# Output projection by column halves, routing tile by tile, and the slot table between the first expert's gate and up

## The reference, cut to what matters

```python
x = x + mixer(rmsnorm(x, norm_mix_w[layer]), ...)        # ends with: return mixed @ w_out
x = x + hierarchical_moe(rmsnorm(x, norm_ffn_w[layer]), ...)

g_logits = hf @ w_router_group + b_router_group          # 4 groups: argmax and softmax weight
e_logits = hf @ w_router_expert + b_router_expert        # 32 experts: 8 in the chosen group
top_v, top_i = lax.top_k(e_in_group, 2)                  # two experts for each token
weights = g_w * jax.nn.softmax(top_v)
a = jax.nn.silu(xblk @ w_expert_gate[e]) * (xblk @ w_expert_up[e])   # width 512
y = a @ w_expert_down[e]                                 # scattered back, times its weight
```

## Time and profile before

| what | us |
|---|---|
| median of three runs | 1530.46 (1529.99 to 1534.29) |
| the profiled execution | 1531.19 |
| its span, first to last instruction | 1529.2 |
| PE busy | 1479.4 (97%) |
| VectorE, ScalarE, GpSimd busy | 824.6, 346.5, 259.4 |
| mean granted TensorE clock | 0.995 |

### The profile page before, as it was taken

One profiled execution on the slowest core, in us unless ns is written; L12 is line 12 of the kernel. 1 busy time (PEld: TensorE's weight loads), 2 busy tenths in 40 slices (PEclk: granted clock), 3 DMA queues, 4 the chain that ended last, 5 costly groups with the idle time before them and its releaser, 6 DMA issues.

```text
span 1529.2 us, 23483 instructions
## 1 busy us (share of the span) xinstructions
PE 1479.4 (97%) x9358; PEld 929.7 (61%) x9358; DVE 824.6 (54%) x1530; ACT 346.5 (23%) x684; POOL 259.4 (17%) x153
## 2 busy tenths in 40 slices
PE   8999999999999999999999999998999999999996
PEld 6877767665555555544488777685655555554453
DVE  2267773555555555454534687635555555555456
ACT  6335563100000000000163354711000000000002
POOL 3343322010000000000133422401000000000001
PEclk9999999999999999999999999999999999999998
DMA  6442144799999999999833321449999999999995
GB/s 206 101 101 69 42 165 179 288 413 422 425 422 424 421 424 421 424 423 422 338 112 94 83 70 28 166 192 392 418 425 420 426 420 423 422 424 421 424 424 223
DMA packets 105773, 464.04 MB, mean 303 GB/s; under 512 B 16616, under 2 KB 59880, under 8 KB 72640
## 3 DMA queue, kind: packets, MB, share of 16 engines
q1 hardware_dynamic: 98208, 449.13, 73.4%
q0 software_dynamic: 6112, 12.32, 2.1%
q10 hardware_dynamic: 1344, 1.05, 0.2%
HBM read 464.32 MB, written 6.29 MB: 308 GB/s over the span
## 4 chain that ended last, share of the span: by engine, by line
PE 79%; DMA 17%; DVE 3%; issue 1%; DVEq 0%; ACTq 0%
PE bank L1755 23%; DMA area<-in_w_expert_up_dram 16%; PE bank L1771 11%; PE bank L1731 7%; PE bank L1578 5%; PE bank L1583 5%; PE bank L1582 5%; PE bank L1648 2%; PE bank L1650 2%; PE bank L1506 2%; PE bank L1649 2%; PE bank L1507 2%; PE bank L1508 2%; PE bank L1598 2%; PE bank L1620 1%; DVE area L1382 1%
## 5 line engine op out<-in xcount | busy, mean ns | idle before, releaser
L1755 PE MATMUL bank<-area 128*64 128x256 f32 x4096 | 461.7, 382 | 17.0 <-DMA area<-in_w_expert_up_dram 15.6
L1755 PEld LDWEIGHTS bank<-area 128*64 128x64 f32 x4096 | 288.5, 137 | 184.6 <-issue 25.8
L1128 DVE TENSOR_TENSOR xres<-xres,bank 128x512 f32<-128x512 f32 x512 | 316.4, 679 | 5.2 <-PE bank L1731 5.2
L1771 PE MATMUL bank<-area 128*64 128x512 f32 x1024 | 233.8, 598 | 6.3 <-DVE area L1382 1.5
L737 POOL DMA_INDIRECT area<-rows,gath x62 | 70.0, 1129 | 739.1 <-PE bank L1723 699.5
L1360 DVE TENSOR_TENSOR area<-area,bank 128x256 f32<-128x256 f32 x64 | 27.0, 421 | 292.9 <-PE bank L1755 292.9
L712 POOL TENSOR_TENSOR w_lo<-area,w_hi 128x1024 fp32r<-128x1024 f32 x55 | 135.1, 2458 | 274.4 <-ACT w_hi L809 274.4
L975 ACT ACTIVATE y_hi<-bank,slot_w 128x512 fp32r<-128x512 f32 x64 | 44.1, 689 | 579.7 <-PE bank L1771 579.7
L1771 PEld LDWEIGHTS bank<-area 128*64 128x64 f32 x1024 | 67.8, 136 | 131.1 <-issue 109.6
L1578 PE MATMUL bank<-h_hi,w_hi 128*128 128x512 f32 x336 | 135.0, 402 | 0.0
L1583 PE MATMUL bank<-h_hi,w_lo 128*128 128x512 f32 x320 | 124.9, 390 | 0.0
(11 more groups left out here) (194 smaller groups left out, 1680.2 us busy)
## 6 DMA issues: line engine op xcount, KB each, us to landing
area<-in_w_expert_up_dram SPq DMA_DIRECT2D x64, 2048.0 KB, 27.4
area<-in_w_expert_gate_dram SPq DMA_DIRECT2D x64, 2048.0 KB, 25.9
area<-in_w_expert_down_dram SPq DMA_DIRECT2D x64, 2048.0 KB, 26.7
area<-in_w_in_dram SPq DMA_DIRECT2D x58, 512.0 KB, 3.9
area<-in_w_out_dram SPq DMA_DIRECT2D x4, 2048.0 KB, 11.2
rows<-area POOLq DMA_DIRECT2D x8, 512.0 KB, 6.7
area<-in_decay_dram SPq DMA_DIRECT2D x2, 1024.0 KB, 6.3
out_dram<-area SPq DMA_DIRECT2D x4, 512.0 KB, 2.9
```

The costliest lines, as they stand in the source:

```text
L1128: tt(xs, xs, bank[4 + i][:, :], ALU.add).then_inc(s_sa[i], 1)
L1755: last = mm(bank[i][SLOTS * half:SLOTS * (half + 1), 0:256], xT[:, c % 4, c // 4, :], w[:, i, c, 256 * half:256 * (half + 1)], start=(c == ...
L1771: last = mm(bank[into][SLOTS * half:SLOTS * (half + 1), :], hx[:, c % 2, c // 2, :], w[:, c, 512 * half:512 * (half + 1)], start=(c == 0), ...
```

## The change

The projection runs by column halves: half 0 of all four tiles, then half 1 of each. Half 0's transposes and logits stand in between; ScalarE copies half 0's transposes and VectorE half 1's. ScalarE sums the squares of each half by itself and scales the rows of all four tiles. When a tile has its logits, `choose` picks its experts by 14 chained VectorE steps on that tile alone; its ranks and its part of the first expert's rows are made on PE as it comes (`rank`, `xb` with a tile number), a tile or two behind. What remains after the last half are steps of tiles 2 and 3, four fillers instead of five and a half, and the count. The slot table follows expert 0's gate. `route`, which prepares it, follows the taking of expert 0's input on VectorE. Buffers move in the area, two of the gather buffers now lie on `xn2` of tile 0, and GpSimd clears them after `xb`. SyncE's part is not changed.

```diff
@@ areas
-XN0 = (PT0, PT0 + D, PB0, PB0 + D)
...
+XN0 = (XG0, OH0, YH0, YH0 + D)
@@ steps
-    out += [("begin", 0, 1), ("mh", 7), ("ml", 7), ("begin", 1, 0), ("begin", 1, 1)]
-
-    out += [("wo", 0, 0), ("wo", 0, 1), ("wo", 1, 0), ("wo", 1, 1)]
-    between = [[("fT", 0, 0)], [("fT", 0, 1)], [("lg", 0, 0)],
-               [("lg", 0, 1)], [("fT", 1, 0)], [("fT", 1, 1)],
-               [("lg", 1, 0)], [("fT", 2, 0), ("lg", 1, 1)], [("fT", 2, 1)],
-               [("lg", 2, 0), ("fT", 3, 0)], [("lg", 2, 1)], [("lg", 3, 0)]]
+    out += [("begin", 1, 0), ("mh", 7), ("ml", 7), ("begin", 2, 0), ("begin", 3, 0)]
+
+    out += [("wo", 0, 0), ("wo", 1, 0), ("fT", 0, 0), ("wo", 2, 0), ("fT", 1, 0), ("lg", 0, 0)]
+    out += [("wo", 3, 0), ("fT", 2, 0), ("lg", 1, 0)]
+    between = [[("fT", 3, 0), ("lg", 2, 0)], [("lg", 3, 0)], []]
+    for t in range(1, NT):
+        between += [[("fT", t - 1, 1)],
+                    [("rank", t - 2), ("lg", t - 1, 1)] if t > 1 else [("lg", t - 1, 1)],
+                    [("xb", t - 2)] if t > 1 else []]
     for n, small in enumerate(between):
-        out += [("wp", 2 + n // 6, n // 3 % 2, n % 3), *small]
+        out += [("wp", n // 3, 1, n % 3), *small]
         if n % 3 == 2:
-            out += [("wo", 2 + n // 6, n // 3 % 2)]
-    out += [("fT", 3, 1), ("lg", 3, 1), ("rank",), ("xb",), ("table",), ("wtab",)]
+            out += [("wo", n // 3, 1)]
+    out += [("rank", 2), ("fT", 3, 1), ("xb", 2), ("lg", 3, 1), ("rank", 3), ("xb", 3), ("count",)]
+    out += [("table",), ("wtab",)]
@@ banks
-            s, b = s[:2], 2 + s[1] % 2
+            s, b = s[:2], (2, 3, 6, 7)[s[1]]
...
-        elif kind == "begin" and s[1]:
-            b = 2 + s[2]
+        elif kind in ("begin", "wp", "wo"):
+            b = s[1] % 2 if s[2] else s[1]
@@ GpSimd
-                nc.gpsimd.memset(at(XG0 + 512, 2 * 512), 0.0).then_inc(s_xgz, 1)
+                pool.wait_ge(s_rows[0], 16 * (layer + 1))
+                is_full(pool, ("xb",), layer)
+                nc.gpsimd.memset(at(XG0, 2 * 512), 0.0).then_inc(s_xgz, 1)
@@ ScalarE
+                    elif kind == "wo" and s[2] == 0:
+                        t = s[1]
+                        is_taken(act, s, layer)
+                        link(nc.scalar.activation(xn2[t][:, 0:512], xres[:, t, 0:512], ACT.Square,
+                                                  accum_out=stat[:, 4 + t:5 + t]))
...
+                    elif kind == "fT" and s[2] == 0:
+                        b, n = result(s, layer)
+                        is_full(act, s, layer)
+                        nc.scalar.activation(hT2[s[1] % 2], bank[b][:, :].rearrange("p (c t) -> p c t", c=4), ACT.Copy
+                                             ).then_inc(freed[b], 2)
@@ VectorE
+            def choose(layer, t):
+
+                g_log, e_log = lgt[:, t, 0:NG], lgt[:, t, NG:].rearrange("p (g e) -> p g e", g=NG)
...
+                link(red(gm, g_log, AX.X, ALU.max))
+                link(stt(out=gfi, in0=g_log, scalar=gm, in1=k("g"), op0=ALU.is_equal, op1=ALU.mult))
+                link(red(own_group, gfi, AX.X, ALU.min))
+                link(ts(pen, k("g"), own_group, NEG, ALU.not_equal, ALU.mult))
+
+                link(tt(near.rearrange("p (g e) -> p g e", g=NG), e_log, each(pen, EPG), ALU.add))
+                link(red(top, near, AX.X, ALU.max))
...
+            def first_rows(layer):
+
+                for kth, found in enumerate((in1, in2)):
+                    link(tt(a12f[:, kth, :, :], over(k("x"), NT), each(found, NE), ALU.is_equal))
+                tt(ed, m2, m1, ALU.subtract).then_inc(s_rin, 1)
+                tt(gs, lgt[:, :, 0:NG], each(gmax, NG), ALU.subtract).then_inc(s_rin, 1)
...
@@ VectorE, the steps
-                        if t and half:
-                            ffn_rows(layer, t - 1)
...
-                        if t == NT - 1:
-                            is_taken(dve, s[:2], layer)
-
-                route(layer)
+                        is_taken(dve, s[:2], layer)
+                        choose(layer, t)
+                    elif kind == "rank":
...
+                        link(nc.vector.tensor_copy(rank[:, t, :], bank[b][:, 0:NE]))
+                        dve.sem_inc(freed[b], 2)
+                        ts(hot_first[t], k("slot")[:, 0:SLOTS], rank[:, t, 0:1], chosen[:, t, 0:1].bitcast(F32),
+                           ALU.is_equal, ALU.mult).then_inc(s_first_hot, 1)
+
+                first_rows(layer)
...
                 take_input(0)
-                for t in range(NT):
-                    dve.wait_ge(s_rows[t], 16 * (layer + 1))
-                b, n = result(("table",), layer)
-                rows_of(layer, ("table",), 0, NE).then_inc(freed[b], 1)
-                weigh(layer)
+                route(layer)
@@ PE
+                        for u in range(t):
+                            mm(o[:, 0:NE], sums[:, 1, :], chosen[:, u, :], start=(u == 0), stop=False)
+                        last = mm(o[:, 0:NE], sums[:, 0, :], chosen[:, t, :], start=(t == 0), stop=True)
+                    elif kind == "count":
+                        for t in range(NT):
+                            last = mm(o[:, 0:NE], sums[:, 1, :], chosen[:, t, :], start=(t == 0), stop=(t == NT - 1))
...
                     if s == ("lg", NT - 1, 1):
-                        is_taken(pe, ("lg", NT - 2), layer)
-                        unread(2, 512, 512, 512, 512, 512, 256)
+                        is_taken(pe, ("wo", NT - 2, 1), layer)
+                        unread(0, 512, 512, 512, 512)
...
                     def ahead(part):
+                        if part and e == 0:
+                            slots_by_expert()
                         if part and e == NE - 1:
                             spread_block(e - 1, (0, 1))
...
-                slots_by_expert(range(0, 3))
                 first_transpose()
-                slots_by_expert(range(3, TOPK * NT))
```

More of the change, by code:

```diff
@@ new lines, in first_rows @@
+            def first_rows(layer):
[3 more added lines that the diff above has]
+                tt(gs, lgt[:, :, 0:NG], each(gmax, NG), ALU.subtract).then_inc(s_rin, 1)
+                b, n = result(("xb",), layer)
+                is_full(dve, ("xb",), layer)
+                for half in range(2):
+                    own = slice(256 * half, 256 * (half + 1))
+                    nc.vector.tensor_copy(xg[0][:, own], bank[b][:, own]).then_inc(freed[b], 1)
@@ L1110, in route @@
                        ).then_inc(s_hots, 1)
-                link(nc.vector.tensor_copy(wbig, each(nfe[:, layer, :].rearrange("p (h j) -> p j h", h=2), SLOTS)))
-                dve.wait_ge(s_rows[1], 16 * (layer + 1))
-                b, n = result(("xb",), layer)
-                is_full(dve, ("xb",), layer)
-                for half in range(2):
-                    own = slice(256 * half, 256 * (half + 1))
-                    nc.vector.tensor_copy(xg[0][:, own], bank[b][:, own]).then_inc(freed[b], 1)
+                tt(hot_exp[:, :, :], a12f.rearrange("p k t e -> p (k t) e"), each(k("row"), NE), ALU.mult
+                   ).then_inc(s_tabin, 1)
+                b, n = result(("count",), layer)
+                is_full(dve, ("count",), layer)
+                nc.vector.tensor_copy(cnt, bank[b][:, 0:NE]).then_inc(freed[b], 2)
+                weigh(layer)
+                for t in range(NT):
+                    dve.wait_ge(s_rows[t], 16 * (layer + 1))
+                b, n = result(("table",), layer)
+                rows_of(layer, ("table",), 0, NE).then_inc(freed[b], 1)
             def add_spread(layer, e, t):
@@ L1462, in _, with table @@
             ident = k("ident")
-            def table(o, hot_col, n, ready=None, part=range(TOPK * NT)):
-                for i in part:
+            def table(o, hot_col, n, ready=None):
+                for i in range(TOPK * NT):
                     if ready is not None and i % NT == 0:
```

182 lines of the change are left out of this document (81 added, 101 removed).

## The result

| | before | after |
|---|---|---|
| median, us | 1531.48 (1529.99 to 1534.29, 6 runs) | 1541.56 (1540.14 to 1544.61, 6 runs) |
| profiled execution / its span | 1531.19 / 1529.2 | 1543.27 / 1541.2 |
| mean granted clock | 0.995 | 0.991 |

The ratio is 1.0066, with a 95% interval of 1.0052 to 1.0081. Forecast was 1528.9, within 1524.5 to 1535.0: wrong in sign, and outside the range. In this part T is read at the issue of the load that waits for it.

A forecast was written before the change was run, and what follows sets the result against it. The experts were taken as bound by the weight stream, which would end 0.8 us earlier in each layer, 1.6 in all: 1531.19 - 1.6 = 1529.6, against the median 1528.9. The range was 1524.5 to 1535.0.

The forecast's parts named there:

- T: The moment the last half is projected, in the first layer: 287.58 us before, forecast at 290.9.
- What bounds the kernel: Experts: bound by the weight stream, 14.8 us per expert against about 13.9 for PE; the stream never pauses.
- The head start: Start of the weight stream: two gate loads leave 20 us earlier; the last load lands 4.1 us earlier, if T stays.
- T does not stay: Projection: rows, ranks, shape changes and bank waits ahead of T move it by 3.3 us, between 2.2 and 4.8.
- the two bank waits: Projection: logits of tiles 0 and 1 wait for banks, about 0.4 us twice, 0.8 in all.
- the 0.4 of the ranks: Projection: ranks newly ahead of T, three matmuls of 0.14 us, cost 0.4 us.
- Tail from T to g: Routing tail behind the projection: 11.5 us instead of 16.2, with 14 choosing steps in 3.0 us.
- g: The first gate matmul, in the first layer: 303.74 us before, forecast at 302.4, 1.3 earlier.
- Table between gate and up: Expert 0: table's 1.2 us on PE free; gather starts at g + 6.0, takes 5.0 us, PE waits 0.7.
- Does the stream run dry: Load needing expert 0's end: issued at 318.0, no pause if by 319.4, so 1.4 us in hand.
- GpSimd's clearing at no cost: Clearing two gather buffers (0.97 us) beside the copy of the first rows: 0 to 1.0 us on g, taken as 0.
- the first (late gather, stream dry, 1536.7): Rival: gather of 9.3 us makes PE wait 5.0; each layer ends 3.1 us later, +6.2, 1536.7; chance 0.14.

The follow-up runs named there:

- e2: The changed kernel with expert 0's down matmuls ahead of the transposes of expert 1's rows: 1536.12 us, ratio 1.0033.
- e12: e2 plus small filler matmuls sized to short PE gaps between T and expert 0's down: 1534.74 us, ratio 1.0026.
- e14: The kernel before with expert 0's down ahead of expert 1's transposes and short gaps filled, without the late table: 1531.41 us, ratio 0.9998.
- e13: The kernel before with the slot table between gate and up, expert 0's down ahead of expert 1's transposes, and short gaps filled: 1532.88 us, ratio 1.0008.
- e5: The changed kernel with the rows of tiles 0 and 1 made behind T, replacing two of four fillers: 1540.53 us, ratio 1.0064.
- e1: The kernel before with only the slot-table matmuls moved between gate and up of expert 0: 1539.36 us, ratio 1.0052.
- e7: The changed kernel with the gate load of expert 3 held until the first gather has landed: 1542.90 us, ratio 1.0078.
- e4: The changed kernel with the slot table and its one-hots made before the first gate again: 1540.09 us, ratio 1.0060.
- e6: e5 with expert 0's down matmuls also ahead of the transposes of expert 1's rows: 1536.87 us, ratio 1.0038.
- e15: e12 with the rows of tiles 0 and 1 moved behind T into the waits there: 1531.73 us, ratio 1.0001.
- e10: e1 with expert 0's down matmuls ahead of the transposes of expert 1's rows: 1536.45 us, ratio 1.0029.
- e8: e6 with extra filler matmuls in the short gaps of the tail behind T: 1537.67 us, ratio 1.0040.

## Why the prediction was wrong

Of the 10.1 us between the medians, 5.4 come back with down ahead of the wait for the gather (e2). Another 1.4 come back with the short gaps filled (e12). The remaining 3.3 are the difference between e12 and e14, two kernels with hardly a pause and without a fall of the clock. e13 stands between these two, as it has the late table and the old order. So 1.5 us are the late table with nobody waiting (e13 against e14: 0.3 and 1.4 us in the stretches from T to the last load), and 1.9 us are the column order (e12 against e13). The last three sizes are rough, since the intervals of e2, e12, e13 and e14 each overlap the next one's. So both theories hold in part: what hung on the wait for the gather was over half of the loss, T's shift a real but smaller part.

- **What bounds the kernel**: right. PE's waits for weights late in each layer were to stay, a little longer; they stayed, but a little shorter, 5.9 us from 600 to 770 and 6.7 from 1350 on, 8.4 and 7.1 before.
- **The head start, 4.1 us if T stays**: right in mechanism and size. The last of the three loads landed at T + 19.2 instead of the T + 18.6 forecast; between e13 and e12, which both have the late table, down first and a full clock, the stretch from T to the last load is 3.7 and 4.6 us shorter.
- **T does not stay, 3.3 us**: mis-sized. It was 4.7, just under the upper end of its bounds: from the issue of expert 1's gate load to T pass 46.8 to 46.9 us in the five profiles with the old order, and 51.5 to 51.6 in the six that have the new one unaltered up to T; the stretch from the last load to the next T, 324.7 to 325.2 us in the former, is 329.3 to 330.0 in the latter. The rows of two tiles were worth 2.2 us a layer by e5 and not 1.8, the two bank waits 0.41 each as forecast, and the choices made the add of a later tile late after all: 0.30 in the first layer and 0.48 in the second at the transposes, which I had taken for covered. One of each, from PE's timeline:

```profile
255.45 1.08 PE L1682 MATMUL bank<-rtw,area 128*128 128x36 f32 x8 [0.41 <-DVE xres L1339]
...
276.27 0.63 PE L1674 MATMUL bank<-kst,xres 128*128 128x128 f32 x4 [0.30 <-DVE xres L1339]
```

  Together with the 0.4 of the ranks these make 3.8 of the 4.7; the other 0.9 was not taken apart. A shift of 4.7 against a head start of 4.1 is a loss of 0.6 us a layer instead of the gain of 0.8: this step alone turned the sign of the sum, though not by much.
- **Tail from T to g, 11.5**: 12.5. The logits left PE 3.9 us after T instead of 3.4, with the steps of tile 2 ahead of them. The 14 steps of choosing took 3.55 us from first to last (0.16 to 0.42 each) and not 3.0. I had priced them at the one row of 0.19; those that take a number per partition are 0.22 to 0.25, and line 1091 took 0.42 here (0.23 for tile 2):

```profile
295.87 0.16 DVE L1088 TENSOR_REDUCE stat<-area 128x1 f32<-128x4 f32 x1
...
296.52 0.42 DVE L1091 TENSOR_SCALAR area<-kst,rowsum 128x4 f32<-128x4 f32 x1
...
299.17 0.25 DVE L1103 SCALAR_TENSOR_TENSOR chosen<-kst,area 128x32 fp32r<-128x32 f32 x1
```

- **Table between gate and up**: this is the step that failed most. The gather's start at g + 6.0 was right to the tenth, also in e1. Its landing, taken at 5.0 because the nearest row was this same gather, was 8.0, 7.1 in e1, 7.3 in e2, and at most 3.3 alone (e7). The nearest row had the right name and not the right company. I wrote that the same one load was in flight and a second joining; by my own sum the gate load of expert 3 was issued ahead of the gather (306.1 and 308.4), where before it came 1.8 us after it (307.46 and 305.67). So the old gather ran mostly while the last load was being finished, and the new one while the gate load of expert 3 ran. That this difference makes 8.0 of 5.0 is a reading of the rows; e7 and e4 show only what the loads as a whole cost. The Trainium skill (DMA: Bandwidth & Descriptors, Queues, rings and completion order) says that an engine takes turns between queue rows packet by packet. By it the sum stayed with the 5.0; it gives no landing time of its own, and no run here shows the turns. The runs show that the loads beside this gather more than double its time. With the down matmuls queued behind the wait for it, that came to 5.4 of the 10.1 us (e2).
- **Does the stream run dry, 1.4 us in hand**: it did, by 5 us. The wait was 3.6 us instead of 0.7, g came 1.7 us late, and the down matmuls took 2.6 us longer for the clock. I wrote that the clock was full throughout, and gave a fall of it no price. With the change PE waits five times between T and the first gate (0.65, 0.23, 0.56, 0.84 and 0.78 us) and 3.6 us behind it, and each fall came behind such waits. But the kernel before has waits of 0.94, 0.88, 0.43 and 0.91 us there, and up to 1.23 in the second layer, with its clock full in both, so its trace could not show this risk; a wait of several microseconds ahead of down, at the high end of my own bounds for the gather, was the place to give it a price.
- **GpSimd's clearing at no cost**: it took 0.95 us beside the copy of the first rows, 0.76 for its two halves; nothing separates it here.
- **The rivals**: the first (late gather, stream dry, 1536.7) named the mechanism, its place and the point from which it decides, about 8.5 us by my T. It ended 5 us short because T came later and because no rival had the clock in it. Its chance of 0.14 was too low: my own line had lone gathers at 7 to 9 us. With the times that came, the last load ahead of the late one was issued at 312.46 and landed 11.3 us later, so 321.3 was soon enough for the next; at full clock and without a wait it would have left at g + 14.8 = 318.9. A landing of over 6.9 us was enough to make a pause.

## What to carry to other kernels

A transfer's time belongs to what runs beside it: when an edit moves a gather, price it with the row whose neighbours are alike, not with the row of its own name. Before a wait is put on an in-order engine, look at what is queued behind it that somebody else needs; here a single swap (down ahead of the transposes) was worth 5.4 us. And where a kernel lives off a full clock, gaps of 0.5 to 0.9 us are not always free: fill them exactly (e12's fillers cut the spread of the runs from 6 to 1.3 us), and measure other edits only then, since an unsteady clock had hidden a gain of 3 us (e2 against e6, then e12 against e15).

## What was unexpected of the hardware

- The granted clock fell to 0.50 for 6 to 7 us with no wait over 0.94 us near it (e10, from 288; the changed kernel, from 1061), in some executions and not in others with the same code: in seven of the eighteen layers counted above, between T and the first gate. In e12 to e15, with these gaps filled or no longer than 0.65 us, it did not fall once in eight layers.
- The first gather landed within 3.3 us alone (e7; 3.3 and 2.8 in e4), after 5.0 beside the end of a load (before, both layers), and after 5.8 to 8.6 behind the moved table, with loads of expert 3 in flight (e8 the shortest, e5 and e6 the longest).
- A filler matmul of 512 columns stands as two instructions and 0.92 us (3.68 for four), at half clock about 1.75 us (e10: its instructions start 0.87 us apart).
